# One slab of a split-precision MLP on eight products instead of seven, a first slab that starts on half its data, and a multiply moved from GpSimd to VectorE

## The reference

```python
h = rmsnorm(x, norm_mix_pre[l])                       # block one, entry
proj = h @ w_in[l]                                    # 1024 x 3584
...
f = jnp.square(jax.nn.relu(h @ w_up[l])) @ w_down[l]  # block one, MLP, 4096 wide
...
h = rmsnorm_2(x, norm_ffn[layer])                     # block two, gated MLP, 2816 wide
x = x + (jax.nn.silu(h @ w_ffn_gate[layer]) * (h @ w_ffn_up[layer])) @ w_ffn_down[layer]
```

## Time and profile before

| | |
|---|---|
| median of three runs | 1400.23 us (1400.18 to 1402.51) |
| the profiled execution | 1401.67 us |
| its span in the trace | 1399.5 us |
| PE busy | 1379.1 us, 99% of the span |
| DVE busy | 1020.1 us, 73% |
| ACT busy | 615.1 us, 44% |
| POOL busy | 419.4 us, 30% |
| mean granted TensorE clock | 0.998 |

### The profile page before, as it was taken

One profiled execution on the slowest core, in us unless ns is written; L12 is line 12 of the kernel. 1 busy time (PEld: TensorE's weight loads), 2 busy tenths in 40 slices (PEclk: granted clock), 3 DMA queues, 4 the chain that ended last, 5 costly groups with the idle time before them and its releaser, 6 DMA issues.

```text
span 1399.5 us, 20853 instructions
## 1 busy us (share of the span) xinstructions
PE 1379.1 (99%) x8375; PEld 1176.2 (84%) x8375; DVE 1020.1 (73%) x1490; ACT 615.1 (44%) x905; POOL 419.4 (30%) x311
## 2 busy tenths in 40 slices
PE   7999999999999999999999999999999999999998
PEld 6888788988988999888878776668888899999997
DVE  6998774757776687578474666774579999998983
ACT  6223344646333434346453437662355343433434
POOL 1040014101333234121132711111235654455532
PEclk9999999999999999999999999999999999999999
DMA  6322223303323323423244212111323232332322
GB/s 201 119 91 91 91 90 124 118 0 96 116 91 92 120 91 100 119 91 98 90 91 121 74 61 61 31 31 61 120 63 94 86 121 91 109 103 91 121 68 83
DMA packets 125792, 129.89 MB, mean 93 GB/s; under 512 B 15777, under 2 KB 110945, under 8 KB 125665
## 3 DMA queue, kind: packets, MB, share of 16 engines
q1 hardware_dynamic: 124560, 124.90, 28.5%
q0 software_dynamic: 992, 3.47, 0.8%
q10 hardware_dynamic: 144, 0.20, 0.0%
HBM read 126.06 MB, written 2.10 MB: 92 GB/s over the span
## 4 chain that ended last, share of the span: by engine, by line
PE 90%; DVE 4%; ACT 2%; issue 2%; POOL 1%; DMA 1%; SPq 0%; ACTq 0%; DVEq 0%; POOLq 0%
PE gemm L643 30%; PE misc L1314 13%; PE gemm L916 9%; PE misc L902 8%; PE gemm L1343 6%; PE gemm L762 3%; PE gemm L1219 2%; PE gemm L930 2%; PE gemm L1357 2%; PE misc L1240 2%; PE misc L1259 1%; PE gemm L846 1%; PE gemm L793 1%; PE gemm L1232 1%; PE misc L1067 1%
## 5 line engine op out<-in xcount | busy, mean ns | idle before, releaser
L643 PE MATMUL gemm<-h_hi,w_hi 128*128 128x512 f32 x520 | 205.0, 394 | 0.0
L643 PE MATMUL gemm<-h_hi,w_lo 128*128 128x512 f32 x520 | 202.5, 389 | 0.0
L643 PE MATMUL gemm<-h_lo,w_hi 128*128 128x512 f32 x520 | 202.5, 389 | 0.0
L2212 DVE TENSOR_TENSOR w_lo<-w_raw,w_hi 128x2048 fp32r<-128x2048 f32 x45 | 103.6, 2303 | 68.8 <-ACT w_hi L1492 68.7
L643 PEld LDWEIGHTS gemm<-h_hi,w_hi 128*128 128x128 f32 x520 | 97.6, 188 | 23.2 <-issue 2.4
L643 PEld LDWEIGHTS gemm<-h_hi,w_lo 128*128 128x128 f32 x520 | 97.6, 188 | 20.4
L643 PEld LDWEIGHTS gemm<-h_lo,w_hi 128*128 128x128 f32 x520 | 97.7, 188 | 19.9 <-issue 0.2
L1492 ACT ACTIVATE w_hi<-w_raw 128x2048 fp32r<-128x2048 f32 x50 | 95.5, 1910 | 5.4 <-PE gemm L762 3.2
L1314 PE MATMUL misc<-ffn_in_hi,ffn_hi 128*128 128x256 f32 x320 | 90.9, 284 | 4.2 <-ACT copy_p L2111 2.6
L1314 PE MATMUL misc<-ffn_in_lo,ffn_hi 128*128 128x256 f32 x320 | 90.5, 283 | 0.0
L1314 PE MATMUL misc<-ffn_in_hi,ffn_lo 128*128 128x256 f32 x320 | 90.5, 283 | 0.0
(11 more groups left out here) (608 smaller groups left out, 4058.2 us busy)
## 6 DMA issues: line engine op xcount, KB each, us to landing
w_raw<-in_w_in SPq DMA_DIRECT2D x62, 512.0 KB, 4.6
mlp_raw<-in_w_down SPq DMA_DIRECT2D x32, 512.0 KB, 4.6
mlp_raw<-in_w_up SPq DMA_DIRECT2D x26, 512.0 KB, 4.7
ffn_raw<-in_w_ffn_gate SPq DMA_DIRECT2D x22, 512.0 KB, 4.7
ffn_raw<-in_w_ffn_up SPq DMA_DIRECT2D x22, 512.0 KB, 4.4
ffn_raw<-in_w_ffn_down SPq DMA_DIRECT2D x16, 512.0 KB, 4.3
w_raw<-in_w_o SPq DMA_DIRECT2D x8, 512.0 KB, 4.0
w_raw<-in_w_out SPq DMA_DIRECT2D x8, 512.0 KB, 4.0
```

Source lines behind the costliest of these rows:

```text
L643: mm = nc.tensor.matmul(bank[:], w(s)[:, kt, col0:col0 + P], x(n), start=first, stop=last)
L2212: V.tensor_tensor(part(lo_of(s), s), part(raw_of(s), s), f(part(hi_of(s), s)), SUB).then_inc(S("lo_done"), SLABS_AT[s])
```

## The change

- **Entry in halves.** Slab 0 comes in two transfers with a semaphore each; ACT makes the high part of each half as it lands. PE runs, for each tile k of the input, the two high-weight matmuls of k and then the two low-weight matmuls of k - 1, which wait for GpSimd's low part tile by tile. Slab 1 gets a routine of its own in which the low weights come last.
- **Joins ahead of splits, block one.** At `up4` the copy of product 1 and the joins U2 and U3 come before the next slab's split; at `up14` the odd low part of the next slab comes after the joins C11 and C21.
- **Second up slab of block two on eight.** `fup1` is a plain slab with two blocks in the ordinary banks. It needs no sums from GpSimd, no `even`/`sums`/`odd` parts and no joins; its high and low parts are made whole (`down_hi`, `down_lo`), and gate and up are multiplied straight from PSUM (`first_gated`).
- **The gate's second factor on DVE.** `norm_gate` is gone; `gate_silu` on DVE makes the silu and multiplies by the norm behind it. GpSimd does only the sums.
- Semaphores with one use are merged under common names (`branch_tanh`, `late_full`, `ln_full`, `fills_ready`).

```diff
-        FFN_PHASES += [(f"fgate{w}", 1, 0 if w else 2), (f"fup{w}", 1, 0 if w else 2)]
+        FFN_PHASES += [(f"fgate{w}", 1, 0 if w else 2), (f"fup{w}", 1, 0 if w > 1 else 2)]
...
+            if c == 0:
+                dst, src = sides.pop(0)
+                sp.dma_start(dst, src).then_inc(S("first_side"), 16)
+            load(c, sides)
...
+        def first_slab():
+
+            def lows(k):
+
+                pe.wait_ge(*((S("first_lo"), k + 1) if k < KT - 1 else (S("lo_done"), 1)))
+                for b in range(2):
+                    nc.tensor.matmul(G[b][:], lo_of(0)[:, k, P * b:P * b + P], HHI[:, k, :], start=False, stop=False)
+
+            for k in range(KT):
+                pe.wait_ge(S("hhi_ready"), k + 1)
+                for b in range(2):
+                    if k == 0:
+                        pe.wait_ge(evac[b], 1)
+                        pe.wait_ge(*((S("hi_done"), 1) if b else (S("first_hi"), 1)))
+                    nc.tensor.matmul(G[b][:], hi_of(0)[:, k, P * b:P * b + P], HHI[:, k, :], start=k == 0, stop=False)
+                if k:
+                    lows(k - 1)
+            lows(KT - 1)
...
+        def second_slab():
+
+            pe.wait_ge(S("hi_done"), 2)
+            for b in range(2):
+                pe.wait_ge(evac[2 + b], 1)
+            for w, x in ((hi_of, HHI), (hi_of, HLO), (lo_of, HHI)):
...
-            for n in (2 * w - 2, 2 * w - 1):
-                for p in ORDER[1 if n == 0 else 0:]:
-                    product(n, p)
+            for n in (GATE_N[w], UP_N[w]):
+                if n is None:
+                    up_block(1, 0)
+                    up_block(1, 1)
+                else:
+                    for p in ORDER[1 if n == 0 else 0:]:
+                        product(n, p)
...
-        split_hi(0)
+        act.wait_ge(S("first_side"), 16)
+        nc.scalar.activation(hi_of(0)[:, :, 0:P], raw_of(0)[:, :, 0:P], ACT.Copy).then_inc(S("first_hi"), 1)
+        act.wait_ge(*raw_full(0))
+        nc.scalar.activation(hi_of(0)[:, :, P:SLAB], raw_of(0)[:, :, P:SLAB], ACT.Copy).then_inc(S("hi_done"), 1)
...
-            if paired:
+            if paired and not closed:
                 up_odd_lo(u + 1)
             up_c11(u)
             up_c21(u)
+            if paired and closed:
+                up_odd_lo(u + 1)
...
-        def silu(w, b):
+        def gate_silu(w, b):
 
             dve.wait_ge(S("ffn_tanh"), 2 * w + b + 1)
-            V.scalar_tensor_tensor(FGATE[:, b, :], SQ[b][:], 1.0, FGATE[:, b, :], ADD, MUL).then_inc(S("gate_silu"), 1)
+            step.inc(V.scalar_tensor_tensor(FGATE[:, b, :], SQ[b][:], 1.0, FGATE[:, b, :], ADD, MUL))
+            step.wait(dve)
+            step.inc(V.tensor_tensor(FGATE[:, b, :], FGATE[:, b, :], RSTD[:], MUL))
...
             if w == 1:
-                first_gated(1)
+                first_gated(0, 1)
                 act_lo(0, 0)
+                join_u2(gate)
+                act_lo(0, 1)
+                join_u3(gate)
+                down_lo(f_ + 1)
+                join_u4_c22(gate)
+                join_c11_c21(gate)
+                join_c12(gate)
+                scale(w)
+                even_lo(f_ + 2)
+                gate_silu(w, 0)
+                gate_silu(w, 1)
+                sums_lo(f_ + 2)
+                first_gated(w, 0)
+                odd_lo(f_ + 2)
+                continue
...
-            silu(w, 0)
-            silu(w, 1)
+            gate_silu(w, 0)
+            gate_silu(w, 1)
...
-        def norm_gate(w, b):
-
-            pool.wait_ge(S("gate_silu"), 2 * w - 1 + b)
-            Q.tensor_tensor(FGATE[:, b, :], FGATE[:, b, :], RSTD[:], MUL).then_inc(S("gate_normed"), 1)
-
         weight_sums(0)
-        for w in range(1, N_W):
-            weight_sums(2 * w - 1)
-            if W_SLAB[w] + 2 in SEVEN_OF:
-                weight_sums(2 * w)
-            for b in range(2):
-                norm_gate(w, b)
-            if w < N_W - 1 and W_SLAB[w] + 2 not in SEVEN_OF:
-                weight_sums(2 * w)
+        weight_sums(1)
+        for w in range(2, N_W):
+            weight_sums(UP_N[w])
+            if w < N_W - 1:
+                weight_sums(GATE_N[w + 1])
```

More of the change, by code:

```diff
@@ L422, in build @@
     W_SLAB = [PH[f"fgate{w}"][0] - SF for w in range(N_W)]
-    SEVENS = [W_SLAB[w] + n for w in range(1, N_W) for n in range(2)]
+    SEVENS = [W_SLAB[w] + n for w in range(1, N_W) for n in range(2) if w + n != 2 or n == 0]
+    GATE_N, UP_N = [[SEVENS.index(W_SLAB[w] + n) for w in range(2, N_W)] for n in range(2)]
+    GATE_N, UP_N = [None, 0] + GATE_N, [None, None] + UP_N
+    JOINS_TO = [sum(7 if x in UP_N else 8 for x in range(n)) for n in range(len(SEVENS))]
     SEVEN_OF = {f_: n for n, f_ in enumerate(SEVENS)}
@@ L680, in run @@
-        def run(name, hi, lo, kts=range(KT), ready=None, lo_slab=0, slabs=None, new_h=None):
+        def first_slab():
[13 more added lines that the diff above has]
+            lows(KT - 1)
+            for k in range(KT):
+                pe.wait_ge(S("hlo_ready"), k + 1)
+                for b in range(2):
+                    mm = nc.tensor.matmul(G[b][:], hi_of(0)[:, k, P * b:P * b + P], HLO[:, k, :], start=False, stop=k == KT - 1)
+                    if k == KT - 1:
+                        mm.then_inc(S("block_full"), 1)
@@ new lines, in second_slab @@
+        def second_slab():
+            pe.wait_ge(S("hi_done"), 2)
+            for b in range(2):
+                pe.wait_ge(evac[2 + b], 1)
+            for w, x in ((hi_of, HHI), (hi_of, HLO), (lo_of, HHI)):
+                if w is lo_of:
+                    pe.wait_ge(S("lo_done"), 2)
+                for b in range(2):
+                    for k in range(KT):
+                        mm = nc.tensor.matmul(G[2 + b][:], w(1)[:, k, P * b:P * b + P], x[:, k, :],
+                                              start=k == 0 and w is hi_of and x is HHI, stop=k == KT - 1 and w is lo_of)
+                    if w is lo_of:
+                        mm.then_inc(S("block_full"), 1)
@@ L681, in run @@
+        def run(name, hi, lo, kts=range(KT), ready=None, lo_slab=0, slabs=None):
             s0, n, _, _ = PH[name]
@@ L683, in run @@
             for s in range(s0 + lo_slab, s0 + lo_slab + n):
-                if new_h and s == s0 + lo_slab:
-                    first_slab(s, 2, *new_h)
-                else:
-                    slab(s, hi, lo, kts, ready)
+                slab(s, hi, lo, kts, ready)
         def mean_rows(src, start, stop, bank=M[0]):
@@ L1869, in r_out @@
             full(m0 + 9 + hd)
-            A_(RG[:, hd, :], G[(m0 + 9 + hd) % 4][:], ACT.Tanh, scale=0.5).then_inc(S("r_tanh"), 1)
+            A_(RG[:, hd, :], G[(m0 + 9 + hd) % 4][:], ACT.Tanh, scale=0.5).then_inc(S("branch_tanh"), 1)
         def level(l):
@@ L1949, in _ @@
         split(15)
[L1950 to L1951 removed]
+        act.wait_ge(S("late_full"), GLA_H + 1)
+        A_(HT[:], M[2][:, 0:P], ACT.Tanh, scale=0.5).then_inc(S("branch_tanh"), 1)
         act.wait_ge(S("hidden_T"), 1)
```

153 lines of the change are left out of this document (68 added, 85 removed).

## The result

The changed kernel takes 1392.2 us (median of four, 1391.31 to 1392.81) against 1400.3 for the kernel before (four runs with the three above, 1400.18 to 1402.51): 8.1 us or 0.6% less, ratio 0.9938, 95% interval 0.9921 to 0.9955. Repeated later against other runs of before it gave 0.9934 (0.9921 to 0.9947). The forecast was 1393.8, 6.4 us less. The first interval spans a gain of 6.3 to 11.1 us and would hold 6.4, the second starts at 7.4; which step of the forecast was off is read from the traces.

The account below looks back on a forecast made before the run. PE was taken to bound the kernel. Entry -2.2, block one -0.4, fup1 -4.05 and factor 0 gave -6.65; restarts +0.25 made it -6.4, so 1393.8 us for the median, range 1391.8 to 1398.8.

Parts of the forecast that it names:

- 42 to 43.5: Block two, first product of fgate1 to first down block of width 2: this many us in place of 46.5.
- Entry, -2.2: Slab 0 at the entry ends 2.2 us earlier, 0.9 from the earlier start and 1.3 from filled holes; bounds 0.9 and 2.5.
- Block one, -0.4: The 0.29 us wait before product 6 of `up15` goes, with the pipe's restart; -0.4 us, 0.3 to 0.5.
- the reorder at `up4`: Block one: PE doesn't wait at `up4`, so worth nothing; another tenth if the join were late.
- fup1 on eight, -4.05: Block two: 6.2 us of stall removed, +0.85 PE price, +0.3 and +1.0 residuals; bounds -5.35 and -2.
- no stall left: Best bound for fup1 on eight in block two: -5.35 us.
- The two residuals, 0.3 and 1.0: Block two: us allowed for late low sums, 0.3 for those of fgate2 and 1.0 for those of fgate3.
- some 1.8 us late: DVE's lateness at the last gate join of width 2, letting GpSimd's fgate3 sums take the port before the silus.
- The factor on DVE, 0: Block two, widths 3 to 10: moving the gate's second factor from GpSimd to DVE changes the time by 0.
- Restarts, +0.25: PE switches between kinds of slab at two more edges; 0.25 us added for restarts.
- More stall left: Rival, chance 0.27: more stall in widths 1 to 3, or part of the entry lost; 1395.5 to 1397.4 us.
- The flip: Rival, chance 0.10: GpSimd's first sum takes the port before the first silu; eight turns cost 5 to 14 us, 1399 to 1408.

Follow-up runs that it names:

- factor_only: The kernel before with only the gate's second factor moved to DVE, fup1 left on seven products: 1400.92 us, ratio 1.0000 to the kernel before.
- silu_later: The changed kernel with the silu pairs behind the joins U4 and C22 of the up slab: 1397.39 us, ratio 0.9970 to the kernel before.
- old_entry: The changed kernel with the entry of the kernel before (whole first slab, one routine for slabs 0 and 1): 1395.62 us, ratio 0.9956 to the kernel before.
- after_again: The changed kernel run once more, nothing altered: 1392.94 us, ratio 0.9934 to the kernel before.
- port_taken: The changed kernel with four subtractions put back on GpSimd at width 0, on a spare buffer: 1395.30 us, ratio 0.9954 to the kernel before.
- copies_first: The kernel before with only the order changed at widths 1 and 2: product 1's copy and join U2 moved ahead: 1403.26 us, ratio 1.0015.
- width1_load: The changed kernel with four extra multiplies on DVE in width 1, ahead of fgate2's low sums: 1397.74 us, ratio 0.9975 to the kernel before.
- four_more: The changed kernel with four more DVE multiplies behind the gated pair in each of eight turns: 1417.39 us, ratio 1.0112 to the kernel before.

## What of the forecast held, and the steps that failed

What bounds the kernel, the four parts and their order of size came out as forecast. The step that failed is the stall left behind fup1: the four slabs took 41.14 us, below the 42 to 43.5 that the forecast gave as its sign.

- **Entry, -2.2: right with a full clock (-2.03), -0.81 in the profiled execution.** Start 0.96 (forecast 0.9), holes 1.08 (1.3). What the step left out is that filling the holes also takes away the cover for slow matmuls.
- **Block one, -0.4: -0.50 alone, -0.52 in the kernel after.** The lower estimate for the reorder at `up4`, nothing, held.
- **fup1 on eight, -4.05: the mis-sized term. It measured -5.36, the bound "no stall left".** The stall removed (6.2) and the price were right: fup1 took 10.90 us, 0.82 more than the 10.08 of a slab on seven, against +0.85 from the rows. By the rule that the Trainium skill gives in "TensorE: Matmul & The Clock Gate", section "Back-to-back issue gap", for an isolated matmul it would be +1.2; the measurement decides for the rows. The two residuals, 0.3 and 1.0, were zero. The step that failed is "in turns with GpSimd's next four sums; I get the sums' low part at 1082.9". In the time of the kernel after that is 1080.0; it came at 1078.57. (The 1083.05 at which PE wants it should have been 1082.97 by the steps of the earlier trace rows, so the slack of this schedule was 0.07 and not 0.15.) GpSimd waited 3.00 us for fup2's raw slab, until 1073.49, and three of the four silu operations ran at 0.68 to 0.69; I had them held. So DVE wasn't "some 1.8 us late" at width 2 either: its first silu there went 0.48 us ahead of GpSimd's first sum, and fgate3's low sums came 1.6 us early. The mechanism behind the 1.0 is real, though: factor_only has it, at 1.65 us.
- **The factor on DVE, 0: right, and its schedule too.** Turned to the time of after, the forecast `gated` pair ends at 1164.65, and it ended at 1164.64. Only the slack was underrated: 1.83 us where I had 0.5, since the low activations at 1166.29 went 0.4 us ahead of GpSimd's sum and took 0.68 in place of 1.78.
- **Restarts, +0.25: nothing.** No distance at the two new edges is longer than its step.
- **The end, no term: -0.8.** The forecast put nothing for the final store. Its landing is 0.8 us shorter in every kernel with fup1 on eight or the factor on DVE.
- **Sum.** With a full clock the parts of the single kernels are -2.03 - 0.50 - 5.37 - 0.8 = -8.7; with the entry at its average of 1.5 they are some -8.2. The medians gave -8.1 and, repeated, -8.8. Against the forecast the two residuals make 1.3 of the difference, the end 0.8, the restarts 0.25 and block one 0.1, and the entry in the stretch at 1.2 GHz gives some 0.7 back on average. That the total is off by only 1.7 us is in part luck.
- **The rivals.** "More stall left" didn't happen. (By its own terms it would have been 1395.1 to 1397.2 and not 1395.5 to 1397.4.) The flip didn't either, in the kernel after, though the margin was 0.26 to 0.65 us; silu_later puts GpSimd's first sum first in every turn and pays 5.5 us, the low end of my 5 to 14, though with the wider slack. It costs 1.8 to 1.9 us only in the two turns where the sum is barely ahead. factor_only has the flip once, with the sum 0.2 us ahead. I called it a loss of one sum per operation, where most of its price is what DVE's lateness meets next.

## What to carry to other kernels

Where two engines alternate on a port, a lateness isn't passed on one to one: list what the late engine meets next, for a raw slab that landed 0.14 us ahead made 2.24 us out of 1.22. An edit that fills the holes of a bound engine was worth 2.0 us with a full clock and about 1 in a slow stretch, so compare kernels by the same stretch at the same granted clock before believing a microsecond. A slab moved to the plain form paid 0.8 us of PE time for 6.2 us of stall, since the work that it takes off the helper engines stood in front of a deadline; moving the copy and one join ahead without taking work off only moved the wait. And compare the last transfer of two kernels as well: here it gave 0.8 us that no edit was meant to give.

## What the runs showed of the hardware

- A stretch of 3.4 us at 1.2 GHz falls into the entry (6 of 14 profiles), one of 3.4 or 6.8 us near 815 us (7 of 14); old_entry has both, after_again and port_taken neither; after and after_again are one program. Its cost is 1.6 us where PE is full (before, at 816), 1.2 in the new entry, and at most 0.1 in the old one, where PE waits for others.
- Long waits of PE came with more of them: 6.8 us at 0.50 after one of 2.7 us (copies_first), 3.4 us at one of 3.2 (width1_load) and at four of the eight of 2.3 to 2.6 (four_more); at those of up to 1.7 us in block two none. What sets the limit between them wasn't tested. A long wait cost 1.4 us (width1_load) or 2.2 (copies_first) above its length.
- DVE operations that read one operand from PSUM (the joins at 0.40 to 0.43, `first_gated` at 0.67 to 0.68) were never held by GpSimd; those with two operands in SBUF were, 0.68 to 1.83 for the silu's 128 x 512. The Trainium skill, "Advanced Engine Details and Errata", section "VectorE Performance Modes", has the sharing of the second port. In the timelines above the two take turns by whole instructions.
- The final store landed 3.56 us after its issue in four kernels and 2.71 to 2.75 in the other ten, the same in both profiles of the changed kernel.
